# Hybrid retention/mLSTM block with experts: a fifth projection pair by seven products, retention packed, two of four weight sums by adding transfers

## The chip, the cores and the metric

One NeuronCore of one Trainium2 chip. The metric is the device time of one launch in microseconds (us). The kernel before took a median of 1027.17 us in 3 runs (1025.9 to 1028.44).

## The reference, cut to what matters

A decoder block on x of 512 tokens by 1024, all in float32. The part that the change touches is the input projection and what its columns feed:

```python
h = rms_norm(x, norm_mix_w)
proj = h @ w_in                     # 512x1024 @ 1024x8200
r_q, r_k, r_v, r_g, m_q, m_k, m_v, m_o, m_i, m_f, gate_r, gate_m = split(proj)
ret = head_rms_norm(retention_chunkwise(rotary(r_q), rotary(r_k), r_v)) * ret_gn_w * silu(r_g)
qk  = silu(causal_depthwise_conv(concat(m_q, m_k)))
hm  = head_rms_norm(mlstm_chunkwise(mq, mk, m_v, m_i, m_f) * sigmoid(m_o)) * mlstm_gn_w
merged = sigmoid(gate_r) * (ret @ w_ret_branch) + sigmoid(gate_m) * (hm @ w_mlstm_branch)
x = x + merged @ w_out
x = x + hierarchical_moe(rms_norm(x, norm_ffn_w))     # 32 experts, 1024 -> 512 -> 1024, two per token
out = rms_norm(x, norm_final_w)
```

Retention and mLSTM each go over 4 heads and 4 chunks of 128 tokens, with keys of 128 and values of 256 columns for each head. A chunk needs the state that the chunk before it left, per head.

## The kernel before, in words

**Blocks and entries.** The projections are made in blocks of 512 weight columns (B_RQ, B_RK, B_RV and so on at the top of the file; 22 blocks, the last six being the two branch matrices and w_out). SyncE brings a block's weights by two loads of 1 MB into a ring of raw tiles (`mix_chunk`, L452). The products keep float32 precision by splitting both sides into a high part and a remainder: for each pair of k-slices, an *entry*, ACT rounds the weights to wh (`mix_head`, L1099) and DVE makes wl = w - wh (`mix_tail`, L1456). Both work LEAD = 3 entries ahead of PE, in a ring of four. A block has four entries; PE makes three products for each piece, wh with hTh, wh with hTl and wl with hTh, 96 matmuls of 512 columns a block (`mix_half`, L630), into four PSUM banks pj. ACT evicts the four banks at the start of the next block (`evict_block`, L1199, and `bank_copy`).

**Fast pairs.** Two neighbouring blocks make a matrix of 1024 by 1024, and four such pairs (FAST: GR, RG, GM, MO) are computed by seven half-size products in place of eight. A product (U_11 to U_T4) works on sums of quadrants of weights and of activations. PE does each as two halves of 12 matmuls of 512 columns, or of 24 with 256 columns where the output is channel-major (`product_half`, L794); halves are counted through by x, 0 to 55. ACT evicts the first result of each quadrant into its home, DVE adds the later ones to it: `upper_left`, `upper_right`, `lower_right` (L1749 to L1767). Each of them frees a bank of PE.

**Weight sums.** Four sums of weight quadrants are needed a pair. Three are DVE's, in two instructions each (`weight_sum`, L1603, called at the halves of SUMS = (2, 3, 7, 8) and around the pair's boundary). The one for U_T3 is made by POOL, through two DMAs of 512 KB that add what they bring to the tile in SBUF (L2100), each issued when the one before has landed. The sums of activations (first21, second, third, fourth: ten terms) are made once by POOL (`combined`, L2076), and split by ACT and DVE (`part_head`, `part_tail`).

**What lies between the matmuls.** The order is written out by hand on each engine: PE's block loop (`block_of`, L741) and pair loop call after every entry or half the small work of that place, and ACT's and DVE's loops (L1224, L1318; L1674, L1778) do the counterpart. Before, the blocks ran RQ, RK, RV, RV+1, MQ, MK, MV, MV+1. The 16 steps of retention (`ret_scores`, `ret_products`; four heads of chunk 0, then chunk 1 and so on) lay one per entry in the four blocks MQ to MV+1; the four steps of each convolution (mq in block MK, mk in block MV: Identity on ACT, three taps on DVE, Sigmoid on ACT, a product on DVE) one per entry; the turned rotary keys (rkT, L1250) in block RV+1; the mLSTM decay matrices dT (DVE L1717) and their exponentials (ACT L1254, L1256) in block MQ; the decayed queries (L1737) in MV+1. The 16 steps of mLSTM attention lay at the halves x = 1 to 27.

After the last pair come the blocks of the two branches and of w_out, the router, and the experts, whose weights (192 loads of 1 MB) SyncE issues as tiles come free. Nothing of that is changed but the addresses of some tiles.

## Time and profile before

| | us |
|---|---|
| median of 3 runs | 1027.17 (1025.9 to 1028.44) |
| profiled execution, its own time | 1025.89 |
| its span, from first to last instruction | 1024.0 |
| PE busy | 999.6 (98%) |
| DVE busy | 505.7 (49%) |
| ACT busy | 316.9 (31%) |
| POOL busy | 108.9 (11%) |

The span is what the trace covers; the execution's own time holds 1.9 us around it. The stages on the time axis: norm and first block to about 40 us; blocks RQ to MV+1 to 219; the four pairs from 219 to 402; branches and w_out to 538; router and tables; the experts from about 590 to 1015.

### The profile page before, as it was taken

To read this page: it belongs to the slowest core of one execution; us is meant where nothing else is said; L and a number is where in the kernel's file an instruction comes from. 1 tells how busy PE (TensorE), PEld (TensorE's weight loads), DVE (VectorE), ACT (ScalarE), POOL (GpSimd) and SP (SyncE) were. 2 spreads that over 40 slices of the span, in tenths; PEclk is the share of its full clock that TensorE was granted. 3 is DMA by queue.
4 is the path that set the end of the run, shared out by engine and by line. 5 is a ranking of instruction groups with operands and counts; after the bars stand their busy time and mean duration, and the time that the engine had idled before them with its cause. 6 is when DMAs were issued, how large, how long until landed. Compare 5 with 4: busy or idle time off the path is not lost.

```text
span 1024.0 us, 13138 instructions
## 1 busy us (share of the span) xinstructions
PE 999.6 (98%) x4941; PEld 648.7 (63%) x4941; DVE 505.7 (49%) x812; ACT 316.9 (31%) x524; POOL 108.9 (11%) x119
## 2 busy tenths in 40 slices
PE   8999999999999999999998999999999999999895
PEld 7888888899988988888885334333333333333333
DVE  6267556567777768645425223333333333332334
ACT  6343564455555656622213000000000000000012
POOL 0688300030000000000000000000000000000000
PEclk9999999999999999999999999999999999999999
DMA  9223221422433525253989899999999999999993
GB/s 330 83 83 125 82 83 42 148 41 73 124 95 116 187 42 168 79 193 102 392 321 367 339 420 420 420 421 420 420 420 420 421 420 419 421 421 421 421 413 142
DMA packets 62579, 268.21 MB, mean 262 GB/s; under 512 B 9456, under 2 KB 9648, under 8 KB 37816
## 3 DMA queue, kind: packets, MB, share of 16 engines
q1 hardware_dynamic: 57464, 257.32, 63.3%
q0 software_dynamic: 4800, 9.98, 4.1%
q8 instruction: 41, 0.67, 0.3%
q14 instruction: 18, 0.15, 0.0%
q10 hardware_dynamic: 256, 0.10, 0.0%
HBM read 267.36 MB, written 4.20 MB: 265 GB/s over the span
## 4 chain that ended last, share of the span: by engine, by line
PE 73%; SPq 17%; DVE 4%; DMA 3%; issue 2%; ACT 1%; DVEq 0%; ACTq 0%
PE pj L648 30%; PE pj L825 13%; PE pj L923 12%; SPq L549 11%; PE pj L949 6%; SPq L546 6%; PE cb L605 3%; DMA raw_moe<-in_w_up_dram 3%; PE cb L959 2%; PE cb L960 1%; PE cb L668 1%; DVE sg L1936 1%; DVE raw_mix L1617 1%; PE cb L697 1%; PE cb L675 1%
## 5 line engine op out<-in xcount | busy, mean ns | idle before, releaser
L923 PE MATMUL pj<-raw_moe,xT 128*64 128x512 f32 x1016 | 227.6, 595 | 4.3 <-DMA raw_moe<-in_w_up_dram 2.2
L1458 DVE TENSOR_TENSOR wl<-raw_mix,wh 128x1024 fp32r<-128x1024 f32 x112 | 145.4, 1300 | 144.5 <-ACT wh L1103 144.1
L923 PEld LDWEIGHTS pj<-raw_moe,xT 128*64 128x64 f32 x1016 | 72.1, 137 | 140.9 <-issue 140.9
L1103 ACT ACTIVATE wh<-raw_mix 128x1024 fp32r<-128x1024 f32 x112 | 118.3, 1059 | 113.5 <-PE pj L648 75.9
L1918 DVE TENSOR_TENSOR x<-x,cb 128x512 f32<-128x512 f32 x120 | 76.9, 682 | 98.5 <-PE cb L960 98.5
L949 PE MATMUL pj<-raw_moe,hf 128*64 128x512 f32 x512 | 116.7, 598 | 1.7 <-ACT hf L1404 1.7
L949 PEld LDWEIGHTS pj<-raw_moe,hf 128*64 128x64 f32 x512 | 35.0, 136 | 66.9 <-issue 66.6
L648 PE MATMUL pj<-wh,hTh 128*128 128x512 f32 x192 | 76.5, 398 | 0.7 <-DVE hTl L1489 0.7
L648 PE MATMUL pj<-wl,hTh 128*128 128x512 f32 x192 | 74.9, 390 | 0.0
L648 PE MATMUL pj<-wh,hTl 128*128 128x512 f32 x192 | 74.8, 390 | 0.0
L1409 ACT ACTIVATE yh<-pj,now 128x512 fp32r<-128x512 f32 x32 | 20.5, 684 | 157.8 <-PE cb L960 143.6
L959 PE MATMUL cb<-yh,hot 128*128 128x512 f32 x124 | 55.2, 445 | 0.0
L1404 ACT ACTIVATE hf<-cb 128x512 f32<-128x512 f32 x16 | 9.6, 598 | 146.1 <-PE cb L605 146.1
L1931 DVE SCALAR_TENSOR_TENSOR sg<-pj,now,sg 128x512 f32<-128x512 f32 x16 | 12.0, 751 | 82.0 <-ACT sg L1400 82.0
L1923 DVE TENSOR_TENSOR xT<-cb,nwc 128x512 f32<-128x512 f32 x32 | 21.9, 687 | 57.2 <-PE cb L605 57.2
L960 PE MATMUL cb<-yl,hot 128*128 128x512 f32 x124 | 49.2, 397 | 0.0
L959 PEld LDWEIGHTS cb<-yh,hot 128*128 128x128 f32 x124 | 23.6, 190 | 29.0 <-issue 26.2
L1400 ACT ACTIVATE sg<-pj,now 128x512 f32<-128x512 f32 x16 | 11.0, 688 | 100.0 <-PE pj L923 90.3
L648 PEld LDWEIGHTS pj<-wh,hTh 128*128 128x128 f32 x192 | 36.1, 188 | 7.9 <-issue 0.9
L648 PEld LDWEIGHTS pj<-wl,hTh 128*128 128x128 f32 x192 | 36.1, 188 | 7.6
L648 PEld LDWEIGHTS pj<-wh,hTl 128*128 128x128 f32 x192 | 36.1, 188 | 6.9
L825 PE MATMUL pj<-hTh,wh 128*128 128x256 f32 x128 | 36.9, 288 | 0.0
(388 smaller groups left out, 1788.2 us busy)
## 6 DMA issues: line engine op xcount, KB each, us to landing
raw_moe<-in_w_gate_dram SPq DMA_DIRECT2D x64, 1024.0 KB, 26.4
raw_moe<-in_w_down_dram SPq DMA_DIRECT2D x64, 1024.0 KB, 26.6
raw_moe<-in_w_up_dram SPq DMA_DIRECT2D x63, 1024.0 KB, 26.4
raw_mix<-in_w_in_dram SPq DMA_DIRECT2D x32, 1024.0 KB, 5.7
raw_mix<-in_w_in_dram POOLq DMA_DIRECT2D x8, 512.0 KB, 5.9
raw_mix<-in_w_ret_branch_dram SPq DMA_DIRECT2D x4, 1024.0 KB, 6.3
raw_mix<-in_w_mlstm_branch_dram SPq DMA_DIRECT2D x4, 1024.0 KB, 5.4
raw_mix<-in_w_out_dram SPq DMA_DIRECT2D x4, 1024.0 KB, 5.1
```

The lines of the kernel that those rows point to most:

```text
L546: sp.dma_start(weights_of(m)[:, :, :].rearrange("p (f c) n -> p f (c n)", f=2), w_down[0][e].rearrange("(a p f) n -> p a f n", a=2, f=2)[: ...
L549: sp.dma_start(weights_of(m)[:, :, :], (w_gate, w_up)[kind][0][e].rearrange("(a p k) n -> p a k n", a=2, k=4)[:, half, :, :]).then_inc(lan ...
L605: return nc.tensor.transpose(o, i, kc[0:k, K_IDENT:K_IDENT + k])
L648: m = nc.tensor.matmul(pj[:, i, :], lhsT, rhs, start=k == 0 and n == 0, stop=k == KD - 1 and n == 2)
L825: m = nc.tensor.matmul(o, lhsT, rhs, start=u in (U_11, U_21, U_T1) and k == 0 and c == 0 and n == 0, stop=k == 3 and n == 2, skip_group_ch ...
L923: mm = nc.tensor.matmul(pj[a * CAP:(a + 1) * CAP, up, :], xT[:, 4 * half + k, a * CAP:(a + 1) * CAP], weights_of(m + a)[:, k, :], start=ha ...
L949: mm = nc.tensor.matmul(pj[a * CAP:(a + 1) * CAP, 2 + c, :], hf[:, 2 * half + f, a * CAP:(a + 1) * CAP], weights_of(m + a)[:, 2 * f + c, : ...
L959: nc.tensor.matmul(bank, hot[:, t * P:(t + 1) * P], yh[:, c * 512:(c + 1) * 512], start=begin, stop=False)
L960: return nc.tensor.matmul(bank, hot[:, t * P:(t + 1) * P], yl[:, c * 512:(c + 1) * 512], start=False, stop=True)
L1103: nc.scalar.activation(wh[:, q % RING, :, :], entry_source(q), ACT.Copy).then_inc(wh_ok, 1)
L1458: V.tensor_tensor(wl[:, q % RING, :, :], entry_source(q), wh[:, q % RING, :, :].bitcast(F32), ALU.subtract).then_inc(wl_ok, 1)
L1918: V.tensor_tensor(part, part, cb[:, 2 + g % 2, :], ALU.add).then_inc(c_add, 1)
```

## The change

It makes MV and MV+1 a fifth pair, ahead of the other four. So there are 70 halves, x = 0 to 69: MV has 0 to 13, GR 14 to 27, RG 28 to 41, GM 42 to 55, MO 56 to 69. The blocks ahead of them are now RQ, RK, MQ, MK, RV, RV+1. The output of the MV pair goes into mva (`home`). For each pair DVE makes the first two sums, and POOL the third and the fourth by four adding transfers in one chain. What lay in the blocks MQ to MV+1 has new places:

- retention: two steps per entry in block RV+1, then one per half x = 0 to 8; its order is now heads 0 and 1 over all chunks, then heads 2 and 3 (`ret_step`);
- the convolution of mq in block MK, beside the turned rotary keys, that of mk in block RV;
- decays at x = 10, 12, 14, 15 on DVE, their exponentials at 11, 13, 15, 16 on ACT, decayed queries at 17, 19, 20, 23 on DVE; attention at 16 halves of x = 20 to 42;
- POOL's ten terms in quarters of 256 columns, and only after the convolutions; `fourth` now ahead of `third`.

```diff
-IN_COLS = [C_RQ, C_RK, C_RV, C_RV + 512, C_MQ, C_MK, C_MV, C_MV + 512, C_RG, C_RG + 512,
+IN_COLS = [C_RQ, C_RK, C_MQ, C_MK, C_RV, C_RV + 512, C_MV, C_MV + 512, C_RG, C_RG + 512,
            C_GR, C_GR + 512, C_GM, C_GM + 512, C_MO, C_MO + 512]
...
-FAST = (B_GR, B_RG, B_GM, B_MO)
+FAST = (B_MV, B_GR, B_RG, B_GM, B_MO)
+F0 = B_MV
...
-SUMS = (2, 3, 7, 8)
+SUMS = (2, 3)
 GATINGS = (5, 6, 11, 12, 14, 15, 18, 24)
-ATTENTION = [1 + (26 * i + 7) // 15 for i in range(16)]
+ATTENTION = [20 + (22 * i + 7) // 15 for i in range(16)]
+ML_FIRST = ATTENTION[0]
+DECAYS = (10, 12, 14, 15)
+DECAY_EXPS = (11, 13, 15, 16)
...
+        raw_first = at("raw_first", 80, [P, 4, 512])
...
+        def ret_step(n):
+
+            return n % 8 // 2, 2 * (n // 8) + n % 2
+
+        def states_by(n):
+
+            return 6 * (n // 8) + min(n % 8 + 1, 6)
...
             def quadrants(p):
 
                 if p == 0:
-                    sp.wait_ge(r_o, 12)
-                else:
-                    sp.wait_ge(wl_ok, fast_entry(p - 1, U_22, 1) + 1)
-                    sp.wait_ge(sum_ok, 6 * (p - 1) + 4)
+                    sp.wait_ge(wl_ok, 4 * F0 - 4)
+                    quadrant(p, U_11, 0, 0)
+                    sp.wait_ge(wl_ok, 4 * F0 - 2)
+                    quadrant(p, U_T3, 0, 1)
+                    sp.wait_ge(mqk_ok, 8)
+                    quadrant(p, U_22, 1, 1)
+                    sp.wait_ge(wl_ok, 4 * F0)
+                    quadrant(p, U_21, 1, 0)
+                    return
+                if p == 1:
+                    sp.wait_ge(r_o, 14)
+                sp.wait_ge(wl_ok, fast_entry(p - 1, U_22, 1) + 1)
+                sp.wait_ge(sum_ok, 4 * p)
                 quadrant(p, U_11, 0, 0)
-                sp.wait_ge(wl_ok, 4 * B_RG - 4 if p == 0 else fast_entry(p - 1, U_T3, 1) + 1)
+                sp.wait_ge(wl_ok, fast_entry(p - 1, U_T3, 1) + 1)
                 quadrant(p, U_T3, 0, 1)
-                if p == 0:
-                    sp.wait_ge(wl_ok, 4 * B_RG - 2)
-                else:
-                    sp.wait_ge(sum_ok, 6 * p)
                 quadrant(p, U_21, 1, 0)
-                sp.wait_ge(wl_ok, 4 * B_RG if p == 0 else fast_entry(p - 1, U_T4, 1) + 1)
+                sp.wait_ge(wl_ok, fast_entry(p - 1, U_T4, 1) + 1)
                 quadrant(p, U_22, 1, 1)
 
...
-                    if b == B_MQ and j == 0:
-                        ret_scores(0)
+                    if b == B_RV + 1:
+                        if j == 0:
+                            ret_scores(0)
+                        else:
+                            ret_products(2 * j - 1)
...
-                    if B_MQ <= b < B_RG:
-                        ret_products(b - B_MQ, j)
-                        if 4 * (b - B_MQ) + j < 15:
-                            ret_scores(4 * (b - B_MQ) + j + 1)
+                    if b == B_RV + 1:
...
+                        if x <= 8:
+                            ret_products(7 + x)
+                        if x <= 7:
+                            ret_scores(8 + x)
+                        if x == ML_FIRST - 1:
...
+            def decay_exps(j):
+
+                if j == 0:
+                    act.wait_ge(gex_in, 1)
+                    nc.scalar.activation(gex[:, :, :], gex[:, :, :], ACT.Exp).then_inc(gex_ok, 1)
+                act.wait_ge(dt_in, j + 1)
+                nc.scalar.activation(dT[:, j, :], dT[:, j, :], ACT.Exp, scale=-1.0).then_inc(dt_ok, 1)
+                for c in range(TT):
+                    m = nc.scalar.activation(gbc[:, j, c * P:(c + 1) * P], gbc[:, j, c * P:(c + 1) * P], ACT.Exp, scale=-1.0,
+                                             bias=gcol[:, 3, 4 * j + c:4 * j + c + 1])
+                m.then_inc(wint_ok, 1)
...
-                    if b == B_MV + 1 and j in (1, 2):
-                        part_head(j - 1)
+                    if b == B_RV + 1 and j >= 2:
+                        part_head(j - 2)
...
+                if x in DECAY_EXPS:
+                    decay_exps(DECAY_EXPS.index(x))
...
-                if n == 3:
-                    dve.wait_ge(wl_ok, fast_entry(p, U_T2, v) + 1)
-                    dve.wait_ge(*fast_landed(p, U_21))
-                dst, term = (U_11, (U_T3, U_22, None, U_21)[n])
+                dst, term = U_11, (U_T3, U_22)[n]
                 ks = slice(2 * v, 2 * v + 2)
...
+                    if b == B_RV + 1 and j >= 1:
+                        ret_output(2 * j - 2)
                     if RING <= q + LEAD < ENTRIES:
...
-                    if b == B_MV + 1:
-                        if j == 0:
-                            dve.wait_ge(mqk_ok, 8)
-                        dve.wait_ge(wint_ok, j + 1)
-                        V.tensor_tensor(gbc[:, j, :], gbc[:, j, :], mqT[:, j, :], ALU.mult).then_inc(wq_ok, 1)
-                        if j == 2:
-                            part_tail(0)
+                    if b == B_RV + 1:
                         if j >= 2:
                             weight_sum(0, 0, j - 2)
+                        if j == 3:
...
+                if x <= 9:
+                    ret_output(6 + x)
+                i = 0 if x == ML_FIRST else after + 1
+                if (x == ML_FIRST or after >= 0) and i < 12:
...
+                if x in DECAYS:
+                    decays(DECAYS.index(x))
+                if x in QUERIES:
+                    queries(QUERIES.index(x))
+                if x == 24:
...
-                    weight_sum(p, (1, 3)[SUMS.index(h) // 2], SUMS.index(h) % 2)
+                    weight_sum(p, 1, SUMS.index(h))
...
-                    m = G.tensor_tensor(dst[:, :, :], (dst if n else first)[:, :, :], term.bitcast(F32), op)
+                    for k in range(4):
+                        m = G.tensor_tensor(dst[:, k, :], (dst if n else first)[:, k, :], term[:, k, :].bitcast(F32), op)
...
+            pool.wait_ge(rqT_ok, TT)
+            pool.wait_ge(mqk_ok, 8)
...
-                pool.wait_ge(sum_ok, 6 * p + 2)
-                for v in range(2):
-                    pool.wait_ge(gd_out, 16 + 16 * (2 * p + v))
-                    pool.dma_start(raw_mix[role(p, U_T3)][:, 2 * v:2 * v + 2, :],
-                                   w_in[0][512 + 256 * v:768 + 256 * v, c0:c0 + 512].rearrange("(k p) n -> p k n", p=P),
-                                   accum_op=ALU.add).then_inc(gd_out, 16)
+                pool.wait_ge(sum_ok, 4 * p + 2)
+                for n, u in enumerate((U_T3, U_T4)):
+                    c0 = IN_COLS[FAST[p] + 1 - n]
+                    for v in range(2):
+                        if u == U_T4:
+                            pool.wait_ge(wl_ok, fast_entry(p, U_T2, v) + 1)
+                        pool.wait_ge(gd_out, 16 + 16 * (4 * p + 2 * n + v))
+                        pool.dma_start(quadrant_place(p, U_T3 if u == U_T3 else U_11)[:, 2 * v:2 * v + 2, :],
+                                       w_in[0][512 + 256 * v:768 + 256 * v, c0:c0 + 512].rearrange("(k p) n -> p k n", p=P),
+                                       accum_op=ALU.add).then_inc(gd_out, 16)
 
```

**ACT at the end of the fourth block.** Before, at the end of block RV+1 (rkT is the turned keys, wh the rounded weights, rvo the evicted banks):

```order
L1103 ACTIVATE wh<-raw_mix_114 128x1024
L1250 ACTIVATE rkT<-cb 128x4x128
L1103 ACTIVATE wh<-raw_mix_112 128x1024
L1250 ACTIVATE rkT<-cb 128x4x128
L1154 ACTIVATE rvo<-pj 128x512 x4
L1232 ACT_TABLE_LOAD
L1232 ACTIVATE gex<-gex 128x48
L1103 ACTIVATE wh<-raw_mix_112 128x1024
```

Now, at the end of block MK (mqT is the convolved query, csg its Sigmoid, convx the evicted banks):

```order
L1135 ACTIVATE wh<-raw_mix_112 128x1024
L1288 ACTIVATE rkT<-cb 128x4x128
L1296 ACTIVATE mqT<-convx,vcol 128x512
L1300 ACTIVATE csg<-mqT 128x512
L1186 ACTIVATE convx<-pj 128x512 x4
L1135 ACTIVATE wh<-raw_mix_112 128x1024
L1296 ACTIVATE mkT<-convx,vcol 128x512
L1300 ACTIVATE csg<-mkT 128x512
```

The evictions of the block's four banks now stand behind the last step of a convolution, which goes over DVE and back.

**DVE around the change from one pair to the next with decays beside it.** Before, at the first halves of the first pair (wl are tails, raw_mix the weight sums, mrg the quadrant sums, rden and Cst belong to attention):

```order
L1531 TENSOR_TENSOR st<-cb,dT 128x128
L1458 TENSOR_TENSOR wl<-raw_mix_115,wh 128x1024
L1617 TENSOR_TENSOR raw_mix_115<-raw_mix_115,raw_mix_112 128x1024
L1754 TENSOR_TENSOR mrg<-pj,mrg 128x2x256
L1458 TENSOR_TENSOR wl<-raw_mix_112,wh 128x1024
L1617 TENSOR_TENSOR raw_mix_115<-raw_mix_115,raw_mix_112 128x1024
L1754 TENSOR_TENSOR mrg<-pj,mrg 128x2x256
L1540 TENSOR_SCALAR rden<-cb,gex 128x1
L1541 TENSOR_TENSOR rden<-cb,rden 128x1
L1542 RECIPROCAL rden<-rden 128x1
L1544 COPY Cst<-cb 128x257
```

Now, at x = 14 to 18; ahead of these rows stand, from the tail of x = 12 on, that tail, a step of dT, the tail of x = 13, a weight sum and the tail of x = 14 (dT are the decays, gbc the decayed query; a `x4` row is one step):

```order
L1777 SCALAR_TENSOR_TENSOR dT<-gbc,gcol,kc 128x128 x4
L1650 TENSOR_TENSOR raw_mix_115<-raw_mix_115,raw_mix_113 128x1024
L1493 TENSOR_TENSOR wl<-raw_mix_115,wh 128x1024
L1777 SCALAR_TENSOR_TENSOR dT<-gbc,gcol,kc 128x128 x4
L1493 TENSOR_TENSOR wl<-raw_mix_115,wh 128x1024
L1650 TENSOR_TENSOR raw_mix_115<-raw_mix_115,raw_mix_112 128x1024
L1793 TENSOR_TENSOR mrg<-pj,mrg 128x2x256
L1493 TENSOR_TENSOR wl<-raw_mix_112,wh 128x1024
L1786 TENSOR_TENSOR gbc<-gbc,mqT 128x512
L1650 TENSOR_TENSOR raw_mix_115<-raw_mix_115,raw_mix_112 128x1024
L1793 TENSOR_TENSOR mrg<-pj,mrg 128x2x256
L1493 TENSOR_TENSOR wl<-raw_mix_112,wh 128x1024
```

Attention has left these halves, and decays and a query have come.

**POOL behind the rotary keys.** Before:

```order
L2079 TENSOR_TENSOR first21f<-hTh 128x1024
L2079 TENSOR_TENSOR first21f<-first21f,hTl 128x1024 x2
L2079 TENSOR_TENSOR secondf<-first21f,hTh 128x1024
L2079 TENSOR_TENSOR secondf<-secondf,hTl 128x1024
L2079 TENSOR_TENSOR thirdf<-hTh 128x1024
L2079 TENSOR_TENSOR thirdf<-thirdf,hTl 128x1024 x2
L2079 TENSOR_TENSOR fourthf<-secondf,hTh 128x1024
L2079 TENSOR_TENSOR fourthf<-fourthf,hTl 128x1024
L2100 DMA raw_mix_113<-in_w_in_dram 128x2x512 x8
```

Now:

```order
L2127 TENSOR_TENSOR first21f<-hTh 128x256 x4
L2127 TENSOR_TENSOR first21f<-first21f,hTl 128x256 x8
L2127 TENSOR_TENSOR secondf<-first21f,hTh 128x256 x4
L2127 TENSOR_TENSOR secondf<-secondf,hTl 128x256 x4
L2127 TENSOR_TENSOR fourthf<-secondf,hTh 128x256 x4
L2127 TENSOR_TENSOR fourthf<-fourthf,hTl 128x256 x4
L2127 TENSOR_TENSOR thirdf<-hTh 128x256 x4
L2127 TENSOR_TENSOR thirdf<-thirdf,hTl 128x256 x8
L2151 DMA raw_mix_113<-in_w_in_dram 128x2x512 x2
L2151 DMA raw_mix_112<-in_w_in_dram 128x2x512 x2
L2151 DMA raw_mix_113<-in_w_in_dram 128x2x512 x2
L2151 DMA raw_mix_115<-in_w_in_dram 128x2x512 x2
```

The terms are cut in four, and each pair has four adding transfers, two into each of two tiles.

## Rows read from the trace of the kernel before

**Rows 1.** The page, busy time of each engine, share of the span, instructions.

```profile
PE 999.6 (98%) x4941; PEld 648.7 (63%) x4941; DVE 505.7 (49%) x812; ACT 316.9 (31%) x524; POOL 108.9 (11%) x119
```

**Rows 2.** The chain of waits: start, us, what.

```profile
443.14 95.25 PE pj L648 x420
...
752.98 3.57 SPq L546
```

**Rows 3.** Stages: us; busy of PE, PEld, DVE, ACT, POOL; clock, DMA, GB/s.

```profile
219.00:402.00 183.00, 182.54 (x1151) 164.93 (x1150) 137.15 (x211) 107.23 (x153) 9.91 (x9) 1.00 0.40 110
...
590.00:749.00 159.00, 157.80 (x716) 62.02 (x712) 53.07 (x84) 14.05 (x22) 7.29 (x17) 1.00 1.01 420
```

**Rows 4.** Timeline of ACT, three places: start, us, engine, line, what.

```profile
108.26 0.60 ACT L1250 ACTIVATE rkT<-cb 128x512 f32<-128x512 f32 x1 [2.04 <-PE cb L605]
108.76 1.57 ACT L1154 ACTIVATE rvo<-pj 128x512 f32<-128x512 f32 x3
...
163.89 0.63 ACT L1268 ACTIVATE csg<-mqT 128x512 f32<-128x512 f32 x1 [3.02 <-DVE mqT L1727]
164.43 1.06 ACT L1154 ACTIVATE convx<-pj 128x512 f32<-128x512 f32 x2
...
174.03 0.81 ACT L1264 ACTIVATE mkT<-convx,vcol 128x512 f32<-128x512 f32 x1
177.87 0.63 ACT L1268 ACTIVATE csg<-mkT 128x512 f32<-128x512 f32 x1 [3.03 <-DVE mkT L1727]
```

**Rows 5.** Timeline of PE: three first matmuls, two neighbours of 256 columns.

```profile
110.83 0.39 PE L648 MATMUL pj<-hTh,wh 128*128 128x512 f32 x1
...
165.40 0.48 PE L648 MATMUL pj<-wh,hTh 128*128 128x512 f32 x1
...
235.60 0.28 PE L825 MATMUL pj<-first,wl 128*128 128x256 f32 x1
235.72 0.28 PE L825 MATMUL pj<-first,wh 128*128 128x256 f32 x1
...
396.18 0.47 PE L825 MATMUL pj<-wh,hTh 128*128 128x512 f32 x1
```

**Rows 6.** Timeline of DVE, the taps of a convolution step.

```profile
175.52 2.32 DVE L1727 SCALAR_TENSOR_TENSOR mkT<-convx,vcol,mkT 128x512 f32<-128x512 f32 x3
```

**Rows 7.** DVE: two groups of 219 to 402 us, then two timeline rows.

```profile
L1458 DVE TENSOR_TENSOR wl<-raw_mix,wh 128x1024 fp32r<-128x1024 f32 x55 | 67.3, 1223 | 43.4 <-ACT wh L1103 43.2
L1617 DVE TENSOR_TENSOR raw_mix<-raw_mix,raw_mix 128x1024 f32<-128x1024 f32 x23 | 28.0, 1217 | 0.0
...
115.31 1.13 DVE L1717 SCALAR_TENSOR_TENSOR dT<-gbc,gcol,kc 128x128 f32<-128x128 f32 x4
...
332.18 0.68 DVE L1754 TENSOR_TENSOR sgm<-pj,sgm 128x512 f32<-128x512 f32 x1
```

**Rows 8.** POOL's adding transfers, two issues and all landings; a DVE tail.

```profile
366.77 1.21 POOL L2100 DMA_DIRECT2D raw_mix<-in_w_in_dram  x1 [31.48 <-DVE raw_mix L1617]
373.04 1.22 POOL L2100 DMA_DIRECT2D raw_mix<-in_w_in_dram  x1 [5.06 <-DMA raw_mix<-in_w_in_dram]
...
DMA to landing us min/median/max: 5.8/5.9/6.0
...
378.31 1.23 DVE L1458 TENSOR_TENSOR wl<-raw_mix,wh 128x1024 fp32r<-128x1024 f32 x1 [1.77 <-ACT wh L1103]
```

**Rows 9.** Waits of PE from 300 to 402 us: total, times, longest.

```profile
PE pj L825 <- DVE sgm L1754: 0.3, 1, 0.3
```

**Rows 10.** Timelines of DVE and POOL where both read SBUF.

```profile
106.25 3.25 DVE L1458 TENSOR_TENSOR wl<-raw_mix,wh 128x1024 fp32r<-128x1024 f32 x1 [0.26 <-ACT wh L1103]
...
106.02 5.74 POOL L2079 TENSOR_TENSOR thirdf<-thirdf,hTl 128x1024 f32<-128x1024 f32 x2
```

**Rows 11.** POOL's adding transfer and SyncE's load while it is under way.

```profile
334.08 1.21 POOL L2100 DMA_DIRECT2D raw_mix<-in_w_in_dram  x1 [5.00 <-DMA raw_mix<-in_w_in_dram]
...
336.88 0.37 SPq L476 DMA_DIRECT2D raw_mix<-in_w_in_dram  x1
```

More of the change, by code:

```diff
@@ L510, in _ @@
             sp.dma_start(bif[:, 1:2], b_f.rearrange("l h -> h l")).then_inc(wg_in, 16)
-            for n in range(MIX_RAW, 2 * B_RG):
+            for n in range(MIX_RAW, 2 * F0):
                 mix_chunk(n)
@@ L830, in product_half @@
                         m.then_inc(pair_used, 1)
-            for b in range(1, B_RG):
+            for b in range(1, F0):
                 block_of(b)
@@ L1350, in _ @@
             turned = {2 * (PRODUCTS * w[0] + w[1]) + w[2]: n[0] for w, n in TURNS.items() if len(w) == 3}
-            for b in range(B_RG):
+            for b in range(F0):
                 evict_block(b - 1)
                 block_of(b)
-            evict_block(B_RG - 1)
-            ret_output(15)
+            evict_block(F0 - 1)
             for p in range(len(FAST)):
@@ L1745, in block_of, with decays, queries @@
                         ml_normed(1 - (b - B_WR), b - B_WR)
-                if b == B_RV:
+                if b == B_MQ:
                     rq_turned(3)
+            def decays(j):
+                if j == 0:
+                    dve.wait_ge(gb_in, 16)
+                for c in range(TT):
+                    m = V.scalar_tensor_tensor(dT[:, j, c * P:(c + 1) * P], gbc[:, j, c * P:(c + 1) * P], gcol[:, 0, 4 * c + j:4 * c + j + 1],
+                                               kc[:, K_NOTYET:K_NOTYET + P], ALU.subtract, ALU.add)
+                m.then_inc(dt_in, 1)
+            def queries(j):
+                if j == 0:
+                    dve.wait_ge(mqk_ok, 8)
+                dve.wait_ge(wint_ok, j + 1)
+                V.tensor_tensor(gbc[:, j, :], gbc[:, j, :], mqT[:, j, :], ALU.mult).then_inc(wq_ok, 1)
             def upper_left(p, s):
-                dve.wait_ge(free[s], B_RG + 4 * p + U_11 + 1)
+                dve.wait_ge(free[s], F0 + 4 * p + U_11 + 1)
                 dve.wait_ge(full[2 + s], full_fast(p, U_21, s))
@@ L1824, in _ @@
             dve.wait_ge(c_in, 48)
-            for b in range(B_RG):
+            for b in range(F0):
                 block_of(b)
-            dve.wait_ge(r_out, 16)
-            dve.wait_ge(gex_ok, 1)
             for p in range(len(FAST)):
```

231 lines of the change are left out of this document (111 added, 120 removed).

## The prediction

> **What bounds the kernel now.** I read the page's busy shares first: PE works 999.6 of 1024.0 us, DVE half of that, ACT a third [rows 1]. So the kernel is TensorE's, but a share over the span doesn't say which wait ends last in a stage; for that I read the chain of waits and the table by stage. The chain is one unbroken run of 420 projection matmuls in 95.25 us late in the mixer, 226.8 ns for each; its first step on SyncE, an expert load, is at 752.98 [rows 2], and most of what follows is such loads. The stage table agrees [rows 3]: from 219 to 402 us PE stands still for 0.46 us in all, at a granted clock of 1.00; from 590 to 749 us PE is busy 157.80 of 159.00 us while the queues already move 420 GB/s. The expert loads start behind the mixer's last weights, so whatever the projection stage saves or loses moves the end by the same amount. The change lies wholly in that stage, so what counts is PE's own time there, plus every instant at which PE stands.
>
> The profiled execution took 1025.89 us (span 1024.0); the runs have a median of 1027.17 (1025.9 to 1028.44). I add to 1025.89 and then 1.28 for the median. About 0.3%, 3.1 us, is what a measurement of this kernel can tell from no change.
>
> **The gain.** MV and MV+1 are regular blocks now, 192 matmuls of 512 columns; as a pair they are 14 halves of 12, 168. 24 x 0.2268 = **-5.44 us**. Retention, attention, conv, decays, gates and turns keep their PE instructions, only their places change: 0 on PE itself.
>
> **A, the end of block MK.** The convolution of mq now lies in block MK, beside the copies of rkT. The order on ACT shows the last conv step ahead of the four bank evictions. Before, the fourth rkT copy ran at 108.26 and evictions followed at once at 108.76 [rows 4], while PE began the next block's first bank at 110.83 [rows 5]. Now, from 108.76 on: Identity 0.81 [rows 4], three taps on DVE 2.32 [rows 6], Sigmoid 0.63, one eviction 0.53 (two took 1.06) [rows 4]: 4.29, so bank 0 is free at about 113.1 and PE stands 113.1 - 110.83 = **+2.3**. Did this chain stall PE before? It ended at 163.89 with evictions from 164.43, and PE wanted its bank at 165.40 [rows 4, 5]: it fitted by 0.44 us, since retention products lay on PE in each entry there, which block MK hasn't. Ends: 0, as at that place; and 2.8, if DVE comes late to the taps as ahead of 177.87, where ACT stood 3.03 after the Identity of 174.03 for taps of 2.32 [rows 4, 6]. I take 2.3, the sum of the parts.
>
> **B, the end of block RV.** The same with the convolution of mk, without a copy of rkT: the ACT-DVE period of conv and head is some 5.1 us against 5.44 (24 matmuls) of an entry, so only the last step hangs over: **+0.6**. Ends 0 and 2.3 (A again).
>
> **C, DVE at the change from pair 0 to pair 1.** Decays and queries, once in regular blocks, stand at x = 10 to 23. The order on DVE from the tail of x = 12 to that of x = 18 is 7 tails at 1.223, 4 sums at 1.217, 3 decays at 1.13, 2 quadrant sums at 0.68 and one query at 0.68 [rows 7]: 18.9 us of work, for which PE leaves two halves of 2.72 and four of 2.88 (24 matmuls of 256 columns, 0.12 apart), 17.0 [rows 5]. PE doesn't stand for the tails, three entries ahead, but for the quadrant sums that free its banks. Of the excess of 1.9 I place some 0.5 in the lead that DVE has at x = 12, and take **+1.4**; ends 0 and 2.0. What is late next is the root at x = 17; nothing on PE waits for it.
>
> **D, the fourth sum by transfers.** Before, DVE added it (two instructions a pair, 1.22 each, which other work mostly covered). Now two more transfers of 512 KB stand in one chain with the third sum's: issue, landing 5.8 to 6.0 us, next issue; 366.77 to 373.04 is 6.27 from one issue to the next [rows 8]. Pair 4 (MO) has no attention now, so its halves are bare. Its first transfer goes out at 366.77 and lands at 372.7, the second goes at 373.04 and lands at 378.9; the third needs the tail of 378.31 (1.23), so it goes at 380.2 (0.65 from event to issue, as ahead of 366.77) and lands at 386.1; the fourth at 386.4 to 392.3 [rows 8]. Then come ACT's head, DVE's tail, and the sums of quadrants and outputs ahead of the last bank: 4.0 us, to 396.4, where PE wants it at 396.18 [rows 5]. **+0.3**. In pair 3 (GM), with halves of 2.88, the same chain ends 0.3 before it is wanted: 0. Pairs 0 to 2 have retention or attention in their halves and more room: 0. Ends: 0, and rival 2.
>
> As to the transfers' price: the eight of before took 5.8 to 6.0 us each [rows 8]. The Trainium skill, "DMA: Bandwidth & Descriptors", section "Anatomy of one DMA — SWDGE (gpsimd) path", fits 2.0 us plus bytes over 436 KB/us, an estimate of 3.2 us for 512 KB; by it D would be 0 and the sum 0.3 lower. The trace disagrees, and these accumulate, which that fit doesn't cover.
>
> **Given back.** The one wait on DVE that PE's rows name from 300 to 402 us, 0.3, is for a quadrant sum [rows 9], behind weight sums on DVE's queue. With one of each pair's three sums off DVE, the pairs' 0.46 us of standing [rows 3] goes: **-0.5**.
>
> **POOL's ten terms** for sums of activations are now quarters, and begin after the convolutions, at about 136 us. Ten at 2.87 are 29 us [rows 10], to 165; ACT takes the last one, third, at x = 4, about 182. 17 us of room: 0. Beside them DVE can be held up: at 106.25 a tail took 3.25 us instead of 1.23, while POOL ran whole terms of 2.87 [rows 10]. Uncut, that would be 2 us for a tail on an entry that leaves DVE 3 us free. The Trainium skill, "SBUF — State Buffer", section "Who interferes with whom", has a rule against putting these side by side: the two engines share a port pair, a DVE instruction with two SBUF inputs and a GpSimd one that reads SBUF hold it for their whole length, and the later one fully blocks. The tail of 106.25 agrees. By it a tail waits for one quarter, 0.7 us, and each DVE instruction with two SBUF inputs may; rival 3 is what that gives at worst.
>
> **Sum:** -5.44 + 2.3 + 0.6 + 1.4 + 0.3 - 0.5 = -1.3; profiled 1024.6, **median 1025.8**. Four fifths of the matmuls' gain is lost at the new boundaries.
>
> **The rivals.**
>
> *1. The boundaries don't stand.* ACT and DVE are free long enough ahead of MK's and RV's ends that the chains start earlier, as they fitted at 165.40, and DVE has a lead at C that I don't see. Then A, B and C shrink to about 1 us together: -5.44 + 1.0 + 0.3 - 0.5 = -4.6, median **1022.5**. For it: PE stood for 0.46 us in 183 [rows 3], at a DVE as busy as it will be. Against: A is a chain behind a copy that itself waits for a turn on PE, so it can't start sooner. Chance 0.22.
>
> *2. Slower: the chained transfers.* Four in series in each pair, where two were, and SyncE's loads of the next pair run beside the later two. After the last landing 4.0 us of work precede PE. At t us more for each, pair 4 is later by 4t, pair 3 by 4t - 0.3: 8t - 0.3. It decides from t = 0.6, total 4.5, net -1.3 + 4.5 = +3.2; with t = 1.0 it is 7.7, net +6.4, median **1033.5**. For it: twelve transfers of 512 KB are added to eight, the later two of each pair where no such transfer ran before. Against: the transfer issued at 334.08 had a load of 1 MB issued beside it at 336.88 [rows 11], and the slowest of all eight took 6.0 us. Chance 0.13.
>
> *3. POOL's quarters and DVE in each other's way.* In 136 to 165 us DVE has some 20 instructions with two SBUF inputs; if each waits half a quarter (0.35), 7 us go on DVE, of which its free half takes up all but some 1.5: median **1027.3**. Chance 0.06.
>
> *4. The change doesn't do what it says*, for instance with fewer matmuls taken away: PE's instructions in the built program are 24 fewer, so 0.01.
>
> **How the numbers follow.** My forecast's case has 0.53; its own range is 1024 to 1028.5. With 0.05 for causes I haven't thought of, the cases make: faster (below 1024.1) rival 1's 0.22 and 0.06 of the forecast's, 0.28; slower (above 1030.3) rival 2's 0.13 and 0.02, 0.15; the same 0.57. All four costs at nothing would be 1021.2, all at their ends with nothing given back 1029.1. The range, 1022.2 to 1029.1, takes in rival 1's value and leaves out rival 2's.
>
> **What would show it.** PE's rows: 24 fewer. At the first matmul of block RV a gap of 2.3 us, released by ACT's eviction of convx; at RV+1 0.6. Around x = 16 to 20 the waits of PE name DVE's sum into mrg, 1.4 us together. In the last pair a wait before x = 13's bank of 0.3, with landings still at 5.8 to 6.0. Wrong if PE waits for a transfer (rival 2), or if the boundaries show under 1 us (rival 1), or if DVE tails between 136 and 165 us take over 1.5 us with a gap on PE behind them (rival 3).

## The result and the profile after

The change made the kernel slower: 1043.16 us median (1042.76 to 1044.68, 4 runs) against 1026.72 of the kernel before in the same session, a ratio of 1.0157 with a 95% interval of 1.0145 to 1.0169. The forecast was 1025.8, its range 1022.2 to 1029.1. The profiled execution has a span of 1041.5 us, 17.5 more than before (the medians differ by 16.4: the profiled execution of the kernel before, 1025.89, is its quickest).

The page of the changed kernel, busy time and granted clock by slices:

```profile
PE 1002.6 (96%) x4917; PEld 648.5 (62%) x4917; DVE 504.2 (48%) x820; ACT 323.9 (31%) x530; POOL 132.9 (13%) x161
...
PEclk9999999999999898999999999999999999999998
```

PE has the 24 matmuls fewer, and yet its busy time is 3.0 us longer than in [rows 1]: in two slices, 338 to 364 and 391 to 417 us, the digit of the clock is not full (a third, the last, is the kernel's end). PE's waits from 40 to 425 us (total, times, longest) name where it stands:

```profile
PE pj L853 <- DVE sgm L1806: 5.2, 1, 5.2
PE pj L853 <- DVE msg L1806: 5.0, 1, 5.0
PE pj L673 <- ACT convx L1186: 2.2, 1, 2.2
PE pj L853 <- DVE sgm L1793: 1.4, 1, 1.4
PE pj L853 <- DVE mrg L1793: 1.0, 2, 0.6
PE pj L673 <- ACT rvo L1186: 0.5, 1, 0.5
PE pj L853 <- ACT mva L1337: 0.4, 1, 0.4
```

Lines 3 and 6 are my terms A and B, line 5 is C; line 7, ACT's first copy at the same boundary, belongs to C too; line 4 is a wait at x = 46 that I had not foreseen. The first two are new in size: the ends of pairs 3 and 4, on DVE's last quadrant sum. DVE isn't slow there. The chain of waits behind the end of pair 3, and its last step at the end of pair 4 (start, us, what):

```profile
340.85 5.88 DMA raw_mix<-in_w_in_dram
...
346.78 0.64 issue
347.42 10.03 DMA raw_mix<-in_w_in_dram
...
357.47 1.06 ACT wh L1135
...
358.56 0.04 DVE wl L1493
...
394.26 10.61 DMA raw_mix<-in_w_in_dram
```

The third adding transfer takes 5.88 us, as those of [rows 8]; the fourth takes 10.03, and at the end of pair 4 it takes 10.61. From the landing on, head, tail and sums need 4.4 us until PE starts at 361.82. What is different about the fourth stands in the timelines of POOL and SyncE of both places (SyncE's row at 347.69 is three loads, two of them at 347.69 and 348.10, the third at 359.81):

```profile
347.42 1.22 POOL L2151 DMA_DIRECT2D raw_mix<-in_w_in_dram  x1 [5.35 <-DMA raw_mix<-in_w_in_dram]
...
347.69 12.48 SPq L496 DMA_DIRECT2D raw_mix<-in_w_in_dram  x3
...
394.13 13.47 SPq L489 DMA_DIRECT2D raw_mix<-in_w_ret_branch_dram  x3
...
394.26 1.22 POOL L2151 DMA_DIRECT2D raw_mix<-in_w_in_dram  x1 [5.37 <-DVE wl L1493]
```

Two loads of 1 MB are issued within 0.7 us of the transfer's issue, at both ends. SyncE waits for the tail of U_T3's last entry, POOL for the third landing (at 393.65 in pair 4; the tail that its row names is not what it waits for), and both come at the same time. No semaphore makes them meet, but it isn't chance either: both count from the tail of U_T2's first half. The third transfer goes out behind it and the fourth 6.6 us later; the loads go out three tails later. In pairs 0 to 2 the three tails take 10.5 to 11.4 us, the loads come 3.5 to 4.8 us behind the fourth transfer, and it lands in 5.8 to 6.3 us. In the barer halves of pairs 3 and 4 they take 7.2 and 6.9 us.

Around these waits, and in the router, the granted clock is low. The table by stretches (columns as in [rows 3]); a mean between 0.50 and 1.00 is of a stretch that is only in part at the lower level:

```profile
356.00:366.00 10.00, 4.84 (x27) 4.64 (x26) 6.08 (x8) 5.25 (x7) 0.00 (x0) 0.66 0.52 175
...
408.00:416.00 8.00, 6.89 (x24) 5.52 (x25) 6.45 (x9) 4.41 (x8) 0.00 (x0) 0.68 0.55 183
...
573.00:579.00 6.00, 6.00 (x40) 2.80 (x39) 1.41 (x9) 1.49 (x2) 1.06 (x1) 0.66 0.67 235
```

After each wait of some 5 us PE comes back at the lower level (1.2 GHz): 0.50 granted from 361.8 to 365.4 and from 409.1 to 413.1. Its matmuls of 512 columns stand 0.43 apart instead of 0.227, those of 256 columns 0.21 instead of 0.12: sixteen of the latter and nine of the former, so the two ends lose 1.7 and 2.0 us more by that.

The sum by places: -5.44 for the matmuls; +15.7 for the named waits, -0.5 for the standing of before; +3.7 for the clock at the two pair ends. That is 13.5, and the first branch matmul comes 14.9 later than before; 1.4 us are not assigned. The router adds 2.4, with the clock at 0.50 from 570.3 to 577.0, where this profile of before has 1.00; from the experts' first matmul on the distance stays within 0.4 us.

### The profile page after: what moved, and what is told of

It reads as the page before. It is cut to its first block, busy times and chain, and to the rows that moved or that the text cites. A ratio compares the mean times of both kernels' runs of the same rounds, so it can differ in the third digit from the quotient of the medians.

```text
span 1041.5 us, 13167 instructions
## 1 busy us (share of the span) xinstructions
PE 1002.6 (96%) x4917; PEld 648.5 (62%) x4917; DVE 504.2 (48%) x820; ACT 323.9 (31%) x530; POOL 132.9 (13%) x161
## 4 chain that ended last, share of the span: by engine, by line
PE 66%; SPq 18%; DVE 6%; DMA 5%; ACT 3%; issue 2%; DVEq 0%; POOL 0%; ACTq 0%; POOLq 0%
PE pj L673 23%; PE pj L853 14%; SPq L574 13%; PE pj L955 11%; PE pj L981 6%; SPq L571 5%; DMA raw_moe<-in_w_up_dram 3%; DMA raw_mix<-in_w_in_dram 3%; PE cb L630 3%; PE cb L991 2%; PE cb L992 1%; DVE wl L1493 1%; ACT wh L1135 1%; DVE mkT L1754 1%; PE pj L635 1%
## 5 line engine op out<-in xcount | busy, mean ns | idle before, releaser
L1135 ACT ACTIVATE wh<-raw_mix 128x1024 fp32r<-128x1024 f32 x116 | 122.3, 1056 | 119.4 <-PE pj L673 67.6
L673 PE MATMUL pj<-wh,hTh 128*128 128x512 f32 x128 | 50.8, 397 | 3.4 <-ACT convx L1186 2.2
L673 PE MATMUL pj<-wl,hTh 128*128 128x512 f32 x128 | 49.9, 390 | 0.0
L673 PE MATMUL pj<-wh,hTl 128*128 128x512 f32 x128 | 49.9, 389 | 0.0
L2151 POOL DMA_DIRECT2D raw_mix<-in_w_in_dram x20 | 24.4, 1218 | 197.1 <-DVE raw_mix L1650 106.9
L853 PE MATMUL pj<-wh,hTh 128*128 128x512 f32 x96 | 39.4, 411 | 5.0 <-DVE msg L1806 5.0
L853 PE MATMUL pj<-hTh,wh 128*128 128x256 f32 x128 | 37.7, 295 | 5.5 <-DVE sgm L1806 5.2
L853 PE MATMUL pj<-wl,hTh 128*128 128x512 f32 x96 | 38.3, 399 | 0.0
```

The lines of the kernel that those rows point to most:

```text
L673: m = nc.tensor.matmul(pj[:, i, :], lhsT, rhs, start=k == 0 and n == 0, stop=k == KD - 1 and n == 2)
L853: m = nc.tensor.matmul(o, lhsT, rhs, start=u in (U_11, U_21, U_T1) and k == 0 and c == 0 and n == 0, stop=k == 3 and n == 2, skip_group_ch ...
L1135: nc.scalar.activation(wh[:, q % RING, :, :], entry_source(q), ACT.Copy).then_inc(wh_ok, 1)
```

## The experiments

The theory, called L in what stands on record: the last adding transfer of a pair is stretched by the two loads that are issued beside it. Its rivals: four transfers in a chain are too long by themselves; or packing and the fifth pair are the cause.

**Loads held back until the last transfer has landed (e1).**

```diff
                 sp.wait_ge(wl_ok, fast_entry(p - 1, U_T3, 1) + 1)
+                sp.wait_ge(gd_out, 16 + 64 * p)
                 quadrant(p, U_T3, 0, 1)
                 quadrant(p, U_21, 1, 0)
...
+                    if m == 0:
+                        sp.wait_ge(gd_out, 16 + 64 * len(FAST))
```

> SyncE's loads of the next pair's U_T3 and U_21 quadrants, and the first load of the branch weights, wait until the fourth adding transfer of the pair has landed. Theory L (the last adding transfer is stretched from 5.8 to 10.0 and 10.6 us because two loads of 1 MB are issued within 0.7 us of it): all transfers land in 5.7 to 6.0 us, PE's waits of 5.2 and 5.0 us at the ends of pairs 3 and 4 shrink to under 1.5 each, the two stretches at a granted clock of 0.66 behind them go (some 4 us), and so does the low stretch in the router if it follows from timing; in all 10 to 14 us faster than the changed kernel, 1030 to 1033, with up to 2 us lost again to later loads. Rival C (four transfers in a chain are too long by themselves): landings stay over 8 us or PE's waits stay above 4 us, time 1041 to 1045.

Measured 1033.25 us (1031.89 to 1034.31), 1.0057 (1.004 to 1.0073) of the kernel before, so 9.9 us of the loss are gone, just under the 10 to 14 expected. All landings and the waits of PE that were left:

```profile
DMA to landing us min/median/max: 5.7/5.8/6.1
```

```profile
PE pj L676 <- ACT convx L1189: 2.2, 1, 2.2
PE pj L856 <- DVE msg L1809: 1.9, 2, 1.7
...
PE pj L856 <- DVE sgm L1809: 0.8, 1, 0.8
```

The chain of four by itself doesn't cost the 5 us, though it isn't free: 1.9 and 0.8 us at the two ends remain. The low clock at the two pair ends is gone, but the router's isn't (0.50 from 561.4 to 564.8), and a new one stands behind the wait of 2.2 us at block RV (0.51 from 114.2 to 117.6).

**One load held, one left (e2).** As above, with the wait ahead of the second load only.

```diff
                 quadrant(p, U_T3, 0, 1)
+                sp.wait_ge(gd_out, 16 + 64 * p)
                 quadrant(p, U_21, 1, 0)
...
                     sp.wait_ge(wl_ok, fast_entry(len(FAST) - 1, U_21, 1) + 1)
+                    sp.wait_ge(gd_out, 16 + 64 * len(FAST))
```

> Only the second of the two loads (U_21, and the second branch load) waits for the fourth adding transfer; one load of 1 MB still goes out beside it. Theory L with sharing in proportion to the bytes in flight: the last landings fall to about 8 us, PE's waits at the two pair ends to 3 us each, time about 1036. If any overlapping load costs the same: landings stay at 10, time about 1043. If one load is harmless, as before at 336.88: landings 6, time as with both loads waiting, and 1 us better for a load that is not late.

1039.78 us (1037.14 to 1042.25), ratio 1.012. POOL's and SyncE's rows at the end of pair 3, then the landing there and the one at the end of pair 4:

```profile
348.47 1.22 POOL L2153 DMA_DIRECT2D raw_mix<-in_w_in_dram  x1 [5.19 <-DMA raw_mix<-in_w_in_dram]
...
348.91 8.61 SPq L497 DMA_DIRECT2D raw_mix<-in_w_in_dram  x2
```

```profile
DMA to landing us min/median/max: 8.7/8.7/8.7
...
DMA to landing us min/median/max: 9.2/9.2/9.2
```

One load, 0.44 us behind the transfer's issue, stretches it by 2.9 us, and one in the same instant (0.01) by 3.4; two stretch it by 4.2 to 4.8. The first costs more than the second, which doesn't fit a share by bytes. One other transfer of this run, at 181.82, took 7.5 us with no load beside it; PE didn't wait for it, and its cause is open.

**Loads later, but not after the landing (e6, e9).** Two runs. In the first SyncE waits for the tail of U_T4's first half:

```diff
-                sp.wait_ge(wl_ok, fast_entry(p - 1, U_T3, 1) + 1)
+                sp.wait_ge(wl_ok, fast_entry(p - 1, U_T4, 0) + 1)
                 quadrant(p, U_T3, 0, 1)
                 quadrant(p, U_21, 1, 0)
...
-                    sp.wait_ge(wl_ok, fast_entry(len(FAST) - 1, U_T4 if m else U_T3, 1) + 1)
+                    sp.wait_ge(wl_ok, fast_entry(len(FAST) - 1, U_T4, 1 if m else 0) + 1)
```

> The two loads that ran into the last adding transfer are issued when the tail of U_T4's first half is written, some 2.5 us after that transfer's issue in place of 0.3 to 0.7. If an adding transfer is harmed only while it starts (as before a load issued 2.8 us after one left it at 6 us), the last landings are 6 to 7 us and the time is near that with the loads held back, 1032 to 1034. If sharing costs as long as both are under way, landings are 8 to 9 us and the time 1037 to 1040.

1030.88 us (1029.08 to 1033.58), landings 6.0 at most. But that tail came later than I had worked out: loads at 353.24 and 353.65 behind a transfer issued at 348.71, so only its last 1.2 us overlapped, and the run couldn't tell its two cases apart. So I hung the wait on PE's progress, which is nearer:

```diff
                 sp.wait_ge(wl_ok, fast_entry(p - 1, U_T3, 1) + 1)
+                sp.wait_ge(*entry_used(fast_entry(p - 1, U_T2, 0)))
                 quadrant(p, U_T3, 0, 1)
...
+                    if m == 0:
+                        sp.wait_ge(*entry_used(fast_entry(len(FAST) - 1, U_T2, 0)))
```

> The two loads behind the last adding transfer of pairs 0 to 3, and the first branch loads, wait for PE to be halfway through U_T2's second half, which was 1.4 to 2.0 us after that transfer's issue in the changed kernel, in place of 0.3 to 0.7; both are still issued while it is under way. If the transfer is only harmed by loads that come in at its start: landings 6 to 6.5 us and 1031 to 1034. If it is harmed by all that goes on before it lands: landings 9.5 to 10.5 and 1041 to 1044.

1029.97 us (1028.76 to 1030.97), ratio 1.0026. At the end of pair 3, with the landing there:

```profile
347.89 1.22 POOL L2154 DMA_DIRECT2D raw_mix<-in_w_in_dram  x1 [5.27 <-DMA raw_mix<-in_w_in_dram]
...
350.10 6.36 SPq L498 DMA_DIRECT2D raw_mix<-in_w_in_dram  x3
```

```profile
DMA to landing us min/median/max: 5.8/5.8/5.8
```

Two loads issued 2.2 and 2.6 us behind the transfer, with 3.6 us of it still to go, cost it nothing: it lands in 5.83 us, and at the end of pair 4, with loads 2.0 and 2.4 us behind, in 5.80. (The slowest of this run, 6.4, is the one of pair 1, whose loads come 5.1 us behind.) The same two loads issued 0.3 and 0.7 us behind it cost 4.2. So it isn't that both are under way: it is whether the loads are issued in the transfer's first instants, while POOL is still at its issue of 1.22 us or just out of it.

The DMA packets show what happens inside. Here q0 is the queue of POOL's transfers and q1 that of SyncE's loads; the numbers are packets, MB and share of the 16 engines. First the changed kernel from the issue of the stretched transfer (347.4) to 352.0, where q0 has no row; then this run from the same issue (347.9) to 352.7; then the changed kernel from 353.0 to 355.5:

```profile
q1 hardware_dynamic: 437, 0.89, 68.5%
...
q0 software_dynamic: 226, 0.46, 62.9%
...
q1 hardware_dynamic: 1, 0.00, 0.5%
...
q0 software_dynamic: 168, 0.34, 74.0%
q1 hardware_dynamic: 146, 0.30, 35.5%
```

An unharmed transfer's first packet starts 1.9 us after its issue. In the changed kernel the first load's packets start before that, at 1.3 us, nearly all of the load's 1 MB goes first, and the transfer's first packet starts only at 4.9 us; then it shares the engines with the second load. In this run it is the loads that wait: their packets start when the transfer's are nearly out, at 4.8 us. So whichever gets its packets in first goes first, and the other waits for it. Why the engines don't take turns from the start, the trace doesn't tell.

The Trainium skill, "DMA: Bandwidth & Descriptors", section "Queues, rings and completion order", has each DMA engine take turns between the queues it has work for, packet by packet. By that alone 512 KB beside 2 MB would be behind by about its own bytes, an estimate of 1.2 us at the 420 GB/s of [rows 3]. The trace agrees with the turns once both queues move packets (168 beside 146 in 2.5 us), but not with the sum: the transfer was behind by 4.2 and 4.8 us with the early loads, and by nothing with the later ones.

**One part of the change alone (e11).** The kernel before, with its four pairs, retention and attention where they were, and the fourth sum by two more transfers:

```diff
-SUMS = (2, 3, 7, 8)
+SUMS = (2, 3)
...
-                    weight_sum(p, (1, 3)[SUMS.index(h) // 2], SUMS.index(h) % 2)
+                    weight_sum(p, 1, SUMS.index(h))
...
-                for v in range(2):
-                    pool.wait_ge(gd_out, 16 + 16 * (2 * p + v))
+                for n, u in enumerate((U_T3, U_T4)):
+                    c0 = IN_COLS[FAST[p] + 1 - n]
+                    for v in range(2):
+                        if u == U_T4:
+                            pool.wait_ge(wl_ok, fast_entry(p, U_T2, v) + 1)
+                        pool.wait_ge(gd_out, 16 + 16 * (4 * p + 2 * n + v))
...
```

> The kernel before with one part of the change alone: its four pairs have the fourth weight sum by two more adding transfers; no fifth pair, retention and attention in their old places. Theory L: the last transfer of the third and fourth pair falls together with two loads and lands after 9 to 11 us, PE waits 3 to 5 us at each of these two ends, clock drops behind them: 1036 to 1041, slower by 10 us or more with no fewer matmuls. If the transfers only hurt because packing left the last pair bare: 1028 to 1030.

1040.8 us (1039.89 to 1042.06), ratio 1.0135 (1.012 to 1.0151): with no other part of the change 14 us of loss. Its waits and landings:

```profile
PE pj L823 <- DVE sgm L1765: 4.7, 1, 4.7
PE pj L823 <- DVE msg L1765: 4.4, 1, 4.4
```

```profile
DMA to landing us min/median/max: 5.6/5.8/10.2
```

At its last two pairs the first load comes 0.3 and 0.1 us behind the last transfer, which lands in 9.6 and 10.2 us; at the two before them it comes 1.6 and 1.4 us behind, and it lands in 5.7. So the harm ends somewhere between 0.44 us, the latest first load that did any in these runs, and 1.4.

**The other parts without it (e3).** The changed kernel with the fourth sum on DVE again, all other parts kept:

```diff
-SUMS = (2, 3)
+SUMS = (2, 3, 7, 8)
...
-                    weight_sum(p, 1, SUMS.index(h))
+                    weight_sum(p, (1, 3)[SUMS.index(h) // 2], SUMS.index(h) % 2)
...
-                for n, u in enumerate((U_T3, U_T4)):
+                c0 = IN_COLS[FAST[p] + 1]
+                for v in range(2):
+                    pool.wait_ge(gd_out, 16 + 16 * (2 * p + v))
...
```

> The fourth weight sum of every pair is made by DVE again, as in the kernel before; the fifth pair and the packed retention stay. Theory L: pair ends are as in the kernel before (waits under 0.5 us), the clock stays at 1.00, boundaries stay at 2.4 and 0.7 us and the DVE waits at the first two pair boundaries grow a little; 1027 to 1030. If the packing and the fifth pair themselves were the cause: above 1035.

1028.87 us (1027.26 to 1030.36, 10 runs), ratio 1.0014 (1.0005 to 1.0024). PE has no wait at the pair ends any more, so DVE had room for these sums. Yet the fifth pair brings nothing: A, B, C and the wait at x = 46 are there as before, and two places cost by the clock. The stretch behind A, and one in the router:

```profile
114.00:117.20 3.20, 3.20 (x9) 2.52 (x8) 1.47 (x2) 2.40 (x4) 0.00 (x0) 0.50 0.00 0
```

```profile
558.00:564.00 6.00, 5.76 (x22) 2.36 (x22) 3.36 (x18) 1.49 (x2) 1.41 (x1) 0.50 0.78 274
```

Behind the same wait of 2.2 us the changed kernel had stayed at 1.00 in that stretch; here it is 1.2 GHz, and eight matmuls are 0.2 us longer each, 1.6 us. The router's low stretch is as long and as low as that of the changed kernel. This profile is of the slowest of the ten runs, 1.5 us above their median, so the median holds less of both.

**The first boundary (e4).** Banks 0 to 2 are evicted between Identity and Sigmoid of the last convolution step:

```diff
+                        if j == 3:
+                            evict_block(b, range(3))
                         act.wait_ge(conv_v, n + 1)
...
-                for i in range(4):
+                if banks is None:
+                    banks = (3,) if p in (B_MK, B_RV) else range(4)
+                for i in banks:
```

> ACT evicts banks 0 to 2 of blocks MK and RV ahead of the last convolution step's Sigmoid, in the time it waits for DVE's taps. The chain that I predicted (Identity, taps, Sigmoid, eviction): PE's gaps of 2.38 us at block RV and 0.67 at RV+1 go to under 0.4 together, 2.5 to 3 us faster than the changed kernel: 1040 to 1041. If the gaps have another cause (late heads or weights) they stay: 1043.

1039.51 us (1037.82 to 1040.79), 3.65 below the changed kernel; both waits, 2.7 us together, are gone from PE's list. The 0.9 beyond them isn't explained by them; in the profiles the router's low stretch is half as long. ACT's timeline at that place:

```profile
108.77 0.81 ACT L1298 ACTIVATE mqT<-convx,vcol 128x512 f32<-128x512 f32 x1
109.48 1.57 ACT L1186 ACTIVATE convx<-pj 128x512 f32<-128x512 f32 x3
111.97 0.63 ACT L1304 ACTIVATE csg<-mqT 128x512 f32<-128x512 f32 x1 [0.93 <-DVE mqT L1758]
```

Sigmoid comes no later than it did, at 111.97 against 112.20 in the changed kernel: the evictions fill ACT's wait for the taps.

**DVE at the change of pairs (e5).** Decays alone moved:

```diff
-DECAYS = (10, 12, 14, 15)
-DECAY_EXPS = (11, 13, 15, 16)
+DECAYS = (9, 10, 11, 12)
+DECAY_EXPS = (10, 11, 12, 13)
```

> The four decay steps move from x = 10, 12, 14, 15 to 9, 10, 11, 12 on DVE, their exponentials from 11, 13, 15, 16 to 10, 11, 12, 13 on ACT, where DVE stands idle for 3.5 us at x = 9; everything else as in the changed kernel. If term C (decays crowd DVE at the change to the second pair) is the cause of PE's gaps of 0.52, 0.72 and 0.58 us there, they go to the level of the kernel before (0.6 together) and the time falls by 1.0 to 1.5 us: 1041.5 to 1042. If other work crowds DVE there (sums, tails), the gaps stay: 1043.

1043.26 us (1041.19 to 1043.98): no change that shows. The gaps at the boundary weren't removed but moved: that of x = 18 fell only from 0.72 and 0.58 to one of 0.70, and one of 0.81 arose at x = 12, where a decay now stood ahead of the quadrant sum (`PE pj L853 <- DVE mva L1806`, 0.7; a gap holds the matmul's usual spacing too). My cause for C, the decays, was only a part of it.

**All mends together (e7, e8, e10, e12).** With loads held, early evictions, decays as in the last run, and attention ending at x = 41:

> Four mends together, adding transfers kept: loads held until the last transfer of a pair has landed; bank evictions ahead of the last Sigmoid; decays at x = 9 to 12; attention ends at x = 41 instead of 42. From 1033.25 with the loads alone: boundaries -3.0 and the clock drop behind the first of them -1.6, decays -1.2, the wait of 1.4 at x = 46 -1.0: 1026.5, no change against the kernel before. If these gaps covered others, 1029 to 1031.

1026.71 us (1025.9 to 1029.63, 10 runs), ratio 1.0002 (0.9993 to 1.0012). And with the fourth sum on DVE in place of the held loads:

> The same three mends beside the fourth sum on DVE (no adding transfer more than before, no load held back). From 1028.87: -3.0, -1.6, -1.2, -1.0: 1022, faster than the kernel before by 0.4 to 0.5 per cent, and by nearly the 5.4 us of the 24 matmuls. If DVE, with 20 sum instructions more, falls behind at the pair boundaries: 1024 to 1026.

1023.35 us (1022.27 to 1024.64), ratio 0.9965 (0.9954 to 0.9977). The wait at x = 46 fell from 1.4 to 0.3. With the evictions or the decays moved alone it had stayed (1.4, 1.3), so of the three edits it is this line's:

```diff
-ATTENTION = [20 + (22 * i + 7) // 15 for i in range(16)]
+ATTENTION = [20 + (21 * i + 7) // 15 for i in range(16)]
```

Then, against the kernel just shown, the decays and the first query at places that keep clear of quadrant sums:

```diff
-DECAYS = (9, 10, 11, 12)
-DECAY_EXPS = (10, 11, 12, 13)
-QUERIES = (17, 19, 20, 23)
+DECAYS = (9, 10, 12, 14)
+DECAY_EXPS = (10, 11, 13, 15)
+QUERIES = (13, 19, 20, 23)
```

> As e8 (fourth sum on DVE, early evictions, attention to x = 41), with decays at x = 9, 10, 12, 14 and the first query at x = 13 in place of 17. With decays moved alone the gap at x = 18 stayed at 0.70 and one of 0.81 appeared at x = 12 behind a decay of x = 11. If the query of x = 17 makes the first and a decay directly ahead of a quadrant sum the second, both fall under 0.3 and the time is 1.0 to 1.2 us below e8: 1022.2. If DVE is short over the whole stretch, the gaps only move: 1023.3.

1022.39 us (1021.64 to 1024.2, 5 runs), ratio 0.9952 (0.9939 to 0.9966), the lowest median of all and faster than both kernels, though its interval overlaps that of the run before it. What PE still waits for from 40 to 425 us:

```profile
PE pj L854 <- DVE mva L1814: 0.7, 1, 0.7
PE pj L854 <- DVE sgm L1801: 0.3, 1, 0.3
```

The gap at x = 18 is gone. Two decays were moved as well, but later, nearer to it, so I put it down to the query; no run moved the query alone. The gap at x = 12 stayed, with a decay still at x = 10 and none at 11, so its cause is still open. Last, all 20 transfers kept, with the loads of e9 and the places of this run:

> The change with all 20 adding transfers, and the four mends: loads 1.4 to 2 us behind the last transfer's issue as in e9, early evictions, decays and query as in e10, attention to x = 41. From e9 at 1030: boundaries -3.0, DVE places -1.5, x = 46 -1.0, the clock drop behind block MK where it comes up to -1.6: 1023.5 to 1024.5. If the chain's length (term D, 0.3 us) is as small as I predicted, it equals e10 (1022.4) within 0.5; if the waits of 1.06 and 1.23 at the ends of pairs 3 and 4 stay or grow as PE comes earlier, it is 2 us above e10.

1025.14 us (1024.44 to 1027.73, 12 runs), ratio 0.9985 (0.9976 to 0.9993): every one of the 20 lands within 6.0 us, with loads 1.8 to 2.3 us behind the last of pairs 3 and 4. The transfers in place of DVE's sums still cost 2.75 us, with waits of 1.4 and 0.3 at the two pair ends.

## Why the prediction was wrong

**Bound and method: right.** What happened up to the first branch matmul moved the rest of the program one to one, apart from the router's clock: 14.9 there, 17.3 at the experts, 17.5 at the end.

**The gain: right.** 24 matmuls fewer; with the fourth sum on DVE and the boundaries mended the first branch matmul comes at 398.0 against 402.2, 4.2 us of the 5.44.

**A and B: right in mechanism and size.** Predicted 2.3 and 0.6; PE's waits were 2.2 and 0.5, released by ACT's evictions as said. The run with early evictions shows the cause. That a wait of this length can bring the lower clock I left out; where it did, it cost 1.6 us more (in four of the seven profiles with the wait).

**C: size near, cause half right.** Predicted 1.4 for the decays; 1.0 of DVE and 0.4 of ACT's first copy were measured. Moving the decays didn't take it away; the run that also moved the query has no wait left at x = 16 to 18. The wait of 1.4 at x = 46 was missed: I followed retention, decays and queries to their new places, but not the end of attention, whose last step at x = 42 now pushes DVE's work at pair 3's start; ending it one half earlier took the wait to 0.3.

**D: the step that failed.** I worked out +0.3 for pair 4 and 0 for pair 3, with every transfer at [rows 8]. It was 5.0 and 5.2 us, and some 4 us of clock. Two things were wrong. I followed POOL's transfers in time, but not SyncE's loads against them: the two would have been seen to go out in the same microsecond. And in rival 2 I took the load at 336.88 beside the transfer of 334.08 [rows 11] as evidence that overlap is harmless. It was issued 2.8 us behind the transfer. The runs show that such a place is harmless (5.8 us at 2.2) and that a first load within 0.5 us isn't (8.7 to 11.3 us, ten transfers in five kernels). A row proves what it shows at its own spacing, no more. Even with no stretch D was too small: pair 3's wait was 0.8 to 1.4 where I had 0, pair 4's 0.3 to 1.9 where I had 0.3. I had the fourth transfer go out 0.3 us behind the third landing and it took 0.6 and 0.7; and the 4.0 us behind the last landing, for which I showed no row, were 4.2 and 4.4.

**Rival 2 was what came**, with 13 in 100 and 1033.5 us. Its place was right, the ends of pairs 3 and 4, and so were the loads that it named; its size was not, with 1043.16 measured. I had spread a small stretch over all transfers, while the last of pair 3 and of pair 4 took 4.2 and 4.8 us more and the rest nothing that shows. The range left it out, and no case held the clock's share.

**Given back and POOL's quarters.** The 0.5 to be given back isn't to be seen: the wait of 0.3 in [rows 9] is 1.4 now, for attention's sake, and it is 0.3 again in the last run, where the transfers are still in place of the sums. POOL's terms ran from 136.3 to 174.0 us, not to 165, and the first adding transfer followed at once; PE didn't wait for either. Rival 3 didn't come: beside the terms DVE's longest tail of weights was 1.75 us, over my mark of 1.5 but far under the 3.25 of [rows 10], and no wait of PE stands beside it.

**What stays open.** The clock in the router. Its low stretch stands in the profiles of the changed kernel (0.50 from 570.3 to 577.0) and of the one with the fourth sum on DVE (0.50 from 557.8 to 564.5), but not in those of the kernel before and of the one with one load held, though PE's waits there are nearly the same in all. It need not follow from the kernel: runs of the kernel before alone lie at 1026 us with a mean clock of 0.998, at 1027.2 with 0.996 and at 1028.3 with 0.993. So one profile beside another can differ by some 2 us with no cause in the change. Open too is why the DMA engines let whichever queue starts first go on, instead of taking turns from the start.

## What to carry to other kernels

When a queue gets more transfers, lay the issue times of *all* queues beside each other, not only the chain's own: a transfer that PE waits for must not share its first microsecond or so with loads that nobody waits for (1.4 us behind was the nearest that did no harm here), and one semaphore on the loads is enough to part them. Test a new helper alone in the old kernel before packing work around it: here 14 of the 16 us came with that part alone. Where PE will wait for 2 us or more, reckon with the lower clock behind the wait too: here it came in four of seven profiles behind 2.2 us, and in all behind 3.4 us and more.
